# PEER expert gathers on GpSimd: four U rows' gathers, then four V rows' gathers, in place of U and V by turns

## What is computed

```
for each of 8 heads:
    scores of 2 x 128 keys -> top 16 of either half -> top 16 of the 256 sums -> 16 expert numbers eidx, softmax gate
    ue  = u_tab[eidx]                       # 16 rows of 1024 floats for each token
    act = gelu(sum_d ue * x)                # 16 dot products for each token
    ve  = v_tab[eidx]                       # 16 rows of 1024 floats for each token
    out += sum_k gate_k * act_k * ve_k
```

## Time and profile before

| | us |
|---|---|
| median of 3 runs | 4653.35 |
| the runs | 4649.70 to 4653.51 |
| the profiled execution | 4650.03 |
| its span | 4648.2 |
| GpSimd busy (gathers, 2560) | 2436.7 (52%) |
| VectorE busy | 2721.4 (59%) |
| TensorE busy | 2217.2 (48%) |
| transfers by the gathers' queue | 1342 MB, 74.9% of 16 engines' span |

### The profile page before, as it was taken

The page is one execution under the profiler, slowest core; times in us unless marked ns, Lnnn a source line. Parts: engine busy times, 40 slices in busy tenths (PEclk is TensorE's granted clock), DMA queues, the critical chain, the costliest instruction groups (busy, mean ns, idle before and its releaser), DMA issues.

```text
span 4648.2 us, 39716 instructions
## 1 busy us (share of the span) xinstructions
PE 2217.2 (48%) x11298; PEld 1061.8 (23%) x11298; DVE 2721.4 (59%) x6959; ACT 1065.9 (23%) x3545; POOL 2436.7 (52%) x2564
## 2 busy tenths in 40 slices
PE   4548565565933433333454378635753332233233
PEld 4444343234511200000341034403420000000000
DVE  1454755775355566666446655376556675666764
ACT  1131232222211112212122222222322221212211
POOL 0023434543265467677346743366357666677675
PEclk7779767667966755565675689867875566556566
DMA  5586778777699999999899997899999999999998
GB/s 184 179 297 238 277 256 308 290 275 270 240 363 384 384 381 403 402 394 399 289 380 394 404 351 275 315 401 389 352 346 400 364 399 370 369 391 398 384 398 335
DMA packets 578410, 1583.75 MB, mean 341 GB/s; under 512 B 50058, under 2 KB 237930, under 8 KB 578066
## 3 DMA queue, kind: packets, MB, share of 16 engines
q0 software_dynamic: 368640, 1342.34, 74.9%
q1 hardware_dynamic: 186514, 217.94, 14.0%
q10 hardware_dynamic: 23040, 20.98, 1.3%
HBM read 1554.62 MB, written 26.44 MB: 340 GB/s over the span
## 4 chain that ended last, share of the span: by engine, by line
PE 25%; DMA 22%; DVE 21%; POOL 12%; issue 12%; ACT 7%; SPq 1%; DVEq 0%; POOLq 0%; ACTq 0%
PE ps_box L925 10%; DMA u_ring<-in_peer_u_dram,idx 10%; POOL v_ring L815 6%; PE ps_v L870 6%; POOL u_ring L805 6%; DVE u_ring L1590 4%; DMA w_slots<-in_w_mod_dram 4%; ACT w_v L1224 4%; DMA v_ring<-in_peer_v_dram,idx_v 3%; PE ps_box L1083 3%; DVE HT L1807 2%; ACT idx_v L1234 1%; DVE onehot L1606 1%; DMA w_slots<-in_peer_keys_dram 1%; PE ps_v L896 1%
## 5 line engine op out<-in xcount | busy, mean ns | idle before, releaser
L1590 DVE CUSTOM_DVE_ANT_0 u_ring<-u_ring,h_cur 128x1024 f32<-128x1024 f32 x1280 | 1534.2, 1218 | 916.2 <-DMA u_ring<-in_peer_u_dram,idx 905.9
L815 POOL DMA_INDIRECT v_ring<-in_peer_v_dram,idx_v x1280 | 1216.0, 950 | 1381.2 <-PE ps_v L870 834.0
L870 PE MATMUL ps_v<-v_ring,w_diag 128*32 128x512 f32 x5120 | 1014.1, 933 | 1657.5 <-DMA v_ring<-in_peer_v_dram,idx_v 1008.7
L805 POOL DMA_INDIRECT u_ring<-in_peer_u_dram,idx x1280 | 1220.5, 954 | 811.2 <-issue 343.7
L870 PEld LDWEIGHTS ps_v<-v_ring,w_diag 128*32 128x32 f32 x5120 | 194.4, 147 | 2390.2 <-issue 1596.5
L925 PE MATMUL ps_box<-HT,w_slots 128*128 128x128 f32 (+2 forms) x1792 | 477.9, 429 | 80.3 <-ACT AR L1444 31.7
L1241 ACT ACT_TABLE_LOAD x79 | 101.4, 1283 | 1164.2 <-DVE act_v L1590 1155.1
L925 PEld LDWEIGHTS ps_box<-HT,w_slots 128*128 128x128 f32 x1792 | 295.5, 210 | 265.0 <-issue 152.7
L1224 ACT ACTIVATE w_v<-w_tok 32x4 f32<-32x4 f32 x1280 | 265.7, 208 | 193.4 <-DVE w_tok L1649 179.4
L1234 ACT ACTIVATE idx_v<-idx 32x4 uint32<-32x4 uint32 x1280 | 265.9, 208 | 16.3 <-ACT AR L1455 0.4
L1083 PE MATMUL ps_box<-w_slots,CAT 128*128 128x256 f32 x640 | 153.2, 402 | 26.2 <-ACT CAT L1429 9.4
(11 more groups left out here) (163 smaller groups left out, 2252.9 us busy)
## 6 DMA issues: line engine op xcount, KB each, us to landing
w_slots<-in_w_mod_dram SPq DMA_DIRECT2D x48, 1024.0 KB, 7.9
w_slots<-in_peer_wq_dram SPq DMA_DIRECT2D x48, 1024.0 KB, 13.0
u_ring<-in_peer_u_dram,idx POOLq DMA_INDIRECT x1280, 7.1
v_ring<-in_peer_v_dram,idx_v POOLq DMA_INDIRECT x1280, 7.2
w_slots<-in_w_in_odd_dram SPq DMA_DIRECT2D x16, 1024.0 KB, 15.0
w_slots<-in_w_in_even_dram SPq DMA_DIRECT2D x14, 1024.0 KB, 7.9
BC<-modrow SPq DMA_DIRECT2D x26, 512.0 KB, 7.3
w_slots<-in_w_out_even_dram SPq DMA_DIRECT2D x12, 1024.0 KB, 11.7
```

Of the source, the lines that this page charges most:

```text
L805: pool.indirect_dma_start(out=u_ring[:, k % NU, :], out_offset=None, in_=u_rows, in_offset=bass.IndirectOffsetOnAxis(ap=idx[:, h % 2, k:k ...
L815: pool.indirect_dma_start(out=v_ring[:, k % NV, :], out_offset=None, in_=v_rows, in_offset=bass.IndirectOffsetOnAxis(ap=idx_v[:, h % 2, k: ...
L870: last = nc.tensor.matmul(ps_v[QUARTER * q:QUARTER * q + QUARTER, 512 * half:512 * half + 512], w_diag[:, c % GROUPS, q, :], v_ring[:, (r ...
L1590: nc.vector.tensor_tensor_reduce(u_ring[:, k % NU, :], u_ring[:, k % NU, :], h_cur[:, :], 1.0, 0.0, ALU.mult, ALU.add, act_v[:, h % 2, k:k ...
```

## The change

In a head step GpSimd issues the four U gathers of a group, then the four V gathers of the same group number, in place of U and V by turns. Each gather keeps its tile, its wait and its place within its own table's sequence. The two lists are only merged in another way. Head step 0, which has no V, and the 16 V gathers behind head step 79 stay as they were. VectorE, ScalarE, TensorE and SyncE keep their programs.

```
             def step(seg, h, first=False):
                 i = seg * 8 + h
                 wait(pool, topk_done, i + 1)
-                for k in range(TOPK):
-                    gather_u(i, h, k)
+                for c in range(GROUPS):
+                    for k in range(4 * c, 4 * c + 4):
+                        gather_u(i, h, k)
                     if not first:
-                        gather_v(i - 1, h - 1, k)
+                        for k in range(4 * c, 4 * c + 4):
+                            gather_v(i - 1, h - 1, k)
```

## The result

| | us |
|---|---|
| before, median of 4 runs | 4651.52 (4649.01 to 4653.51) |
| after, median of 4 runs | 4588.94 (4571.82 to 4593.14) |
| ratio | 0.9859, 95% interval 0.9833 to 0.9885 |
| span of the profiled execution | 4648.2 before, 4584.6 after |

The change makes the kernel 1.4% faster. The forecast was 3.4%, 4494 us. The time lies outside the forecast's own range of 4450 to 4535 us, and inside the wider one, 4385 to 4592 us, only by 3 us. The direction was right and the size was less than half. In the kernel after the change every line behind 822 stands two lines lower (L1592 is the dot, L872 the V sum, L1651 the row weights).

A forecast was written before the change was run, and what follows sets the result against it. The prediction took the transfers, with GpSimd's issue right behind, as the bound. From 4650.0 us it took 61 for PEER alone and 98 beside mixing, then added 3.3 for the median: 4494 us, range 4450 to 4535.

The forecast's parts named there:

- What bounds the kernel: PEER alone: transfers bound it at 410 GB/s, GpSimd's issue right behind, with one stop a step at a V gather.
- Part one, the head of the queue: Ordinary steps of PEER alone: 7.4 us of slack removes the 3.0 us V wait; 89 us were no gap left.
- a landing beyond 11 us: Sign that the forecast is wrong: gathers land later than 11 us after issue, so the V waits come back.
- Part two, the segments' ends: Six segment ends and the loops' seams keep idle transfers, 28 us in all, leaving 61 us for PEER alone.
- So the 7.2 us stay: Behind a segment's end U(i,8) still waits 7.2 us above the usual gap, since the last V gather keeps its place.
- Part three, beside mixing: Head steps beside mixing: earlier U gathers shorten the dots' waits for U tiles, 294 us in all, and gain 98 us.
- the third that was taken: Beside mixing, the share of the dots' 294 us of U waits counted as gain: 98 us.
- The check from the other side: Beside mixing, V groups behind a stop complete 3.7 us sooner; a third of some 80 stops makes 98 us.
- (1): Only PEER alone gains, nothing comes back beside mixing: 4592 us, chance 0.14.
- (2): Mixing gains two thirds, since each shortened stop makes the rows behind it early too: 4396 us, chance 0.16.
- (3): The transfers are full already, so the time stays at about 4648 us, chance 0.06.
- (4), V behind U: Beside mixing, V gathers stand behind U gathers that wait for dots, so groups complete later: 4700 us, chance 0.06.

The follow-up runs named there:

- e4: Kernel before, but with four V gathers first, then four U, in the head steps of PEER alone and all of both loops: 4750.0 us, ratio 1.0214.
- e3: Changed kernel, with the last V group issued ahead of the last U group in each segment's first head step: 4569.6 us, ratio 0.9832.
- e1: Kernel before, with four U then four V only in PEER-alone steps and all of both loops, including the mixing of steps 17 to 20: 4611.4 us, ratio 0.9916.
- e2: Kernel before, with four U then four V only in head steps 0 to 13, 32 to 36, 42 to 45, 50 to 53: 4625.1 us, ratio 0.9945.
- e6: Changed kernel, with four PEER rows in place of two per pair of heads beside layer 0's score pieces of blocks 2 to 4: 4553.4 us, ratio 0.9792.
- e9: Kernel before, U and V by turns, with four PEER rows per pair of heads beside layer 0's score pieces of blocks 2 to 4: 4621.7 us, ratio 0.9950.
- e11: Changed kernel, last V group first at segment starts, more PEER rows beside the score stages of layers 0 and 1: 4519.2 us, ratio 0.9717.

## Why the prediction was wrong, point by point

**What bounds the kernel: right.** The chain from the last dot over the top 16, the weights and the sum to V row 8 was the wait of a step of PEER alone, and the transfers stood behind it. The changed kernel moves 408 to 409 GB/s in three of the five stretches, where 410 was read as the ceiling from two dots. The ordinary steps of the last stretch take 39.7 to 44.7 us, 41.1 on average, where 41 to 41.8 was forecast, and the last stretch moves 399 GB/s where over 400 was the sign.

**Part one, the head of the queue: right.** The wait is gone or short, and e4 shows that the place does it: the same bursts with V first cost 103 us. The estimate of the V ring's cycle (12.1 us of 16.1) was good too. It went wrong in taking the landing as fixed. GpSimd issues each 1.24 us and the transfers take 1.28, so with no wait left the queue grows by about 1.3 us a step (an estimate: 32 x 0.04) until the ring's 16.1 us stop it, at a landing of 16.1 - 4.4 = 11.7 us. The steps fit: three or four at GpSimd's pace, and then short V waits again. The prediction had named this as a sign of being wrong, a landing beyond 11 us that brings the V waits back.

**Part two, the segments' ends: the term that was mis-sized.** "So the 7.2 us stay" failed. In the last stretch they became 12 to 13, because the sum of the last V tile begins 11.8 us after the tile's issue and the end of the segment waits for it. e3 took that wait back to 7.5 us by issuing the last V group 4 places earlier. With V row 8 keeping 2 us as forecast, an end step should have become 3.7 us shorter. The three in the last stretch, 54.2, 54.4 and 51.7 us before, take 57.0, 55.4 and 54.7, which is 4.7 to 6.7 us more than that. At six ends this makes some 36 us (an estimate from these three), more than the whole shortfall of PEER alone: 61 us forecast, 42 in the trace. In e1 the same stretches gave 51 us, and 16 were lost again beside mixing.

**Part three, beside mixing: the step that failed.** The forecast was 98 us. The trace has 20, e2 has 34 in the stretches with mixing and 22 in its whole time. The U waits did fall, by 114 us and so more than the third that was taken, but a wait that goes is no time that is won on engines that run in a fixed order. The sum lacked the step "what is late next" for this part, which it had for part one. Next were the GELU on ScalarE (55 us; e2 shows that they come with this half, and in e6 the time fell as they fell), the modulation's pieces (25 us, in e1's half), the segments' ends and TensorE's pieces at L985 (8 us each). That is 96 of the 114 us. A row for the first was there before: 28.98 us of "issue" at one instruction, a wait without a releaser's name, for which the sum had no term.

**The check from the other side** ("a V group behind a stop is complete 3 places sooner") used the same third for the share on the path and was no check.

**The rivals.** (1) gave the right time, 4592 us, by the wrong sum: it had 61 alone and nothing beside, and the runs have 35 and 22. (2) is out. (3) is out: 409 GB/s is held for 506 us. In one stretch it may hold: in head steps 17 to 20 the DMA share was 1.01 before and is 1.00 now, and the stretch did not become shorter; no run tests this. (4), V behind U, is not seen where it would count: TensorE's waits for V tiles beside mixing went from 92 to 79 us. Its sign was seen, though: GpSimd's waits for dots beside mixing rose from 131 to 554 us. The prediction had named that as what would prove it wrong, and it was mostly the same idle time under another name: all its gaps there went from 944 to 928 us.

**What stays open:** what the order of e3 is worth; how much of e6's gain needs the changed order (e9 doesn't tell); why the waits for the modulation's pieces grew in head steps 17 to 20; and whether the 18 us of the waits' balance and the 20 us of the trace agree by more than luck, since the changed kernel's own runs spread over 21 us.

## What to carry to other kernels

Where an in-order queue serves two rings, put the gather that waits longest behind those that could go, and count its place against the chain that releases it; the order of a merge can be worth more than its bursts. Longer queues are not free: here, once nothing stopped the issuer, the median landing went from 7.2 to 10.7 us, and the ends of the last stretch paid for it (12 to 13 us at U row 8 in place of 7). The worth of a stall removed on one engine is known only after the next wait of the same engine has been read, the nameless ones too, and the place of work in the fixed programs (e6, e11) can be worth more than the queue's order.

## What the runs showed of the hardware

Random rows of 4 KB come in at 409 GB/s for 506 us on end, at a DMA share of 1.03. The Trainium skill ("DMA: Bandwidth & Descriptors", Specifications) gives about 358 GB/s as a core's HBM limit, worked out there as half of a stack's 716; this trace doesn't agree, with one core at work it goes beyond. The median time from issue to landing of a V gather is 7.2 us with turns, 8.6 with pairs and 10.7 with fours, while the stretches of PEER alone move 388 to 409 GB/s in the first and the last: the rate hardly tells how deep the queue is, the landings do.
